# Attention values multiplied with tokens on partitions, normalised afterwards and transposed back, in a two-block transformer kernel

## The reference, cut to what matters

```python
q = apply_rope(rms_norm(q.reshape(B, T, 8, 64), qn_g), cos, sin)     # 8 heads of 64
k = apply_rope(rms_norm(k, kn_g), cos, sin)                          # one key head for all
score = einsum('bqhk,bqh->bqk', relu(q_idx . k_idx), w_idx * scale)  # the indexer
_, sel = lax.top_k(where(visible, score, NEG_INF), 64)
logits = einsum('bqhd,bqkd->bqhk', q, k[sel]) * 64 ** -0.5
p = softmax(where(valid, logits, NEG_INF), axis=-1)
attn = einsum('bqhk,bqkd->bqhd', p, v[sel])                          # one value head for all
y_a = einsum('bte,ed->btd', attn * silu(gate_a), w_a)
```

## Time and profile before

| | us |
|---|---|
| median of 3 runs | 1325.65 |
| lowest, highest | 1323.81, 1327.27 |
| the profiled execution | 1322.05 |
| its span | 1320.3 |
| PE busy | 1278.1 (97%) |
| PE weight loads busy | 1221.1 (92%) |
| POOL busy | 1007.3 (76%) |
| DVE busy | 694.1 (53%) |
| ACT busy | 668.7 (51%) |

### The profile page before, as it was taken

One profiled execution on the slowest core, in us unless ns is written; L12 is line 12 of the kernel. 1 busy time (PEld: TensorE's weight loads), 2 busy tenths in 40 slices (PEclk: granted clock), 3 DMA queues, 4 the chain that ended last, 5 costly groups with the idle time before them and its releaser, 6 DMA issues.

```text
span 1320.3 us, 24716 instructions
## 1 busy us (share of the span) xinstructions
PE 1278.1 (97%) x10187; PEld 1221.1 (92%) x10187; DVE 694.1 (53%) x1293; ACT 668.7 (51%) x1192; POOL 1007.3 (76%) x774
## 2 busy tenths in 40 slices
PE   6999999999999999999999998899999999999997
PEld 6988889988889999998999988899999889999997
DVE  5567647657656344411787688854145435344412
ACT  5455546455555544444555565565446445544532
POOL 4655658866559899987789866668899757899894
PEclk9999999999999999999999999999999999999999
DMA  6433435444335555555456533344556534555562
GB/s 234 144 117 124 128 113 174 153 138 144 116 117 192 170 191 188 189 184 186 130 165 201 163 119 123 126 130 158 182 188 216 165 103 154 177 191 181 186 193 79
DMA packets 57792, 209.05 MB, mean 158 GB/s; under 512 B 6352, under 2 KB 7632, under 8 KB 57424
## 3 DMA queue, kind: packets, MB, share of 16 engines
q1 hardware_dynamic: 57680, 207.48, 48.7%
HBM read 206.41 MB, written 1.05 MB: 157 GB/s over the span
## 4 chain that ended last, share of the span: by engine, by line
PE 86%; DVE 9%; ACT 2%; issue 1%; DMA 1%; SPq 0%; DVEq 0%
PE bank L338 26%; PE bank L340 25%; PE bank L339 25%; PE bank L802 2%; DVE ar L1546 1%; ACT whi L303 1%; PE bank L593 1%; PE bank L810 1%; DVE ar L1567 1%; DVE rows L395 1%; DVE ar L1680 1%; DVE ar L1696 1%; PE bank L817 1%; DMA raw<-w_dram 1%; PE bank L1988 1%
## 5 line engine op out<-in xcount | busy, mean ns | idle before, releaser
L311 POOL TENSOR_TENSOR wlo<-raw,whi 128x512 fp32r<-128x512 f32 x770 | 1007.1, 1339 | 296.7 <-ACT whi L303 296.3
L338 PE MATMUL bank<-xh,whi 128*128 128x256 f32 (+1 forms) x2024 | 586.4, 290 | 15.1 <-DVE xl L377 10.2
L340 PE MATMUL bank<-xh,wlo 128*128 128x256 f32 (+1 forms) x2024 | 575.8, 284 | 0.0
L339 PE MATMUL bank<-xl,whi 128*128 128x256 f32 (+1 forms) x2024 | 575.5, 284 | 0.0
L303 ACT ACTIVATE whi<-raw 128x1024 fp32r<-128x1024 f32 x387 | 399.0, 1049 | 40.4 <-DMA raw<-w_dram 20.2
L338 PEld LDWEIGHTS bank<-xh,whi 128*128 128x128 f32 x2024 | 386.5, 191 | 24.7 <-issue 15.2
L340 PEld LDWEIGHTS bank<-xh,wlo 128*128 128x128 f32 x2024 | 386.9, 191 | 0.0
L339 PEld LDWEIGHTS bank<-xl,whi 128*128 128x128 f32 x2024 | 385.7, 191 | 0.5
L338 PE MATMUL bank<-yh,whi 128*128 128x256 f32 (+1 forms) x1000 | 286.0, 286 | 0.3 <-DVE yl L1870 0.3
L340 PE MATMUL bank<-yh,wlo 128*128 128x256 f32 (+1 forms) x1000 | 283.6, 284 | 0.0
L339 PE MATMUL bank<-yl,whi 128*128 128x256 f32 (+1 forms) x1000 | 283.4, 283 | 0.0
(11 more groups left out here) (245 smaller groups left out, 1169.3 us busy)
## 6 DMA issues: line engine op xcount, KB each, us to landing
raw<-w_dram SPq DMA_DIRECT2D x387, 512.0 KB, 3.8
h<-x_dram SPq DMA_DIRECT2D x2, 544.0 KB, 6.4
cst<-con_dram SPq DMA_DIRECT2D x1, 1049.0 KB, 10.6
ar<-mem_dram SPq DMA_DIRECT2D x1, 1024.0 KB, 5.9
out_dram<-h SPq DMA_DIRECT2D x4, 256.0 KB, 2.7
cst<-con_dram SPq DMA_DIRECT2D x1, 134.0 KB, 3.8
prm<-par_dram SPq DMA_DIRECT2D x1, 131.0 KB, 4.4
```

Of the source, the lines that this page charges most:

```text
L311: return e.tensor_tensor(wlo[:, q, c0:c1], raw[:, i % NRAW, c0:c1], whi[:, q, c0:c1].bitcast(F), ALU.subtract)
L338: e.matmul(o, wh, xhi, start=(i == 0), stop=False)
L339: e.matmul(o, wh, xlo, start=False, stop=False)
L340: m = e.matmul(o, wl, xhi, start=False, stop=(i == len(feed) - 1))
```

## The change

Values and probabilities swap roles in the product: the transposed probabilities are the stationary operand (128 columns), the values the moving one (64 columns), and the output has the 128 query tokens on partitions and all eight heads side by side in the 512 columns of one bank. The probabilities are no longer multiplied by the reciprocals; one DVE operation divides the 128x512 result by the sums (a reciprocal of 8 columns, broadcast over 64), into the new buffer `K.o`. PE transposes that in four 128x128 blocks into a bank `oT`; one DVE operation multiplies by the gate in place in PSUM, one ACT copy makes the high part, one DVE subtraction the low part. Since the transposes of the probabilities wait for the exponential alone, transposes and value products both move one step earlier.

```diff
@@ attend_tensor
         for s in range(8):
-            if s == 4:
+            if s == 3:
                 ob = side_.take(e, "ob", l, t)
-            for hh in (range(2 * s - 8, 2 * s - 6) if s >= 4 else ()):
-                pt, half = K.PT.at(l, t, hh), 64 * (hh % 2)
+            for hh in (range(2 * s - 6, 2 * s - 4) if 3 <= s < 7 else ()):
+                pt = K.PT.at(l, t, hh)
                 e.wait_ge(*s_out.of("pt", l, t, hh))
                 for i, (vi, _, kn) in enumerate(kcs):
-                    m = e.matmul(ob[half:half + 64, 128 * (hh // 2):128 * (hh // 2) + 128], K.V[0:kn, vi, 0:64],
-                                 pt[0:kn, i, :], start=(i == 0), stop=(i == nn - 1))
+                    m = e.matmul(ob[:, 64 * hh:64 * hh + 64], pt[0:kn, i, :], K.V[0:kn, vi, 0:64], start=(i == 0),
+                                 stop=(i == nn - 1))
                 m.then_inc(*piece.done("av", l, t, hh))
-            for hh in (range(2 * s - 6, 2 * s - 4) if 3 <= s < 7 else ()):
+            for hh in (range(2 * s - 4, 2 * s - 2) if 2 <= s < 6 else ()):
                 o = side_.take(e, "pT", l, t, hh)
                 side_.give(("pT", l, t, hh), (s_out, ("pt", l, t, hh)))
-                e.wait_ge(*v_step.of("p", l, t, hh))
+                e.wait_ge(*s_step.of("exp", l, t, hh))
...
+            if s == 7:
+                side_.give(("ob", l, t), (v_step, ("o", l, t)))
+                o = side_.take(e, "oT", l, t)
+                side_.give(("oT", l, t), (v_low, ("y", l, t)))
+                e.wait_ge(*v_step.of("o", l, t))
+                for b in range(4):
+                    m = e.transpose(o[:, 128 * b:128 * b + 128], K.o[:, 128 * b:128 * b + 128], ident)
+                m.then_inc(*piece.done("oT", l, t))
             yield
-        side_.give(("ob", l, t), (v_step, ("y", l, t, 3)))
@@ attend_scalar
-            for hh in (2 * s - 6, 2 * s - 5) if 3 <= s < 7 else ():
+            for hh in (2 * s - 4, 2 * s - 3) if 2 <= s < 6 else ():
                 pt, o = K.PT.take(e, l, t, hh), side_.at("pT", l, t, hh)
...
-        for b in range(4):
-            y, _ = K.y(b, 0)
-            e.wait_ge(*v_step.of("y", l, t, b))
-            e.activation(y[:, c0:c0 + 128], K.tmp.at("y", l, t, b)[:, 0:128], ACT.Copy).then_inc(*s_high.done("y", l, t, b))
+        e.wait_ge(*v_step.of("y", l, t))
+        e.activation(K.y4(0, c0), side_.at("oT", l, t).rearrange("p (a b) -> p a b", b=128), ACT.Copy).then_inc(
+            *s_high.done("y", l, t))
@@ attend_vector
-            if 2 <= s < 6:
-                hs = slice(2 * s - 4, 2 * s - 2)
-                e.wait_ge(*s_step.of("exp", l, t, 2 * s - 3))
-                e.reciprocal(K.rs[:, hs], K.sm[:, hs]).then_inc(*v_step.done("rs", l, t, s - 2))
-                e.wait_ge(*v_step.of("rs", l, t, s - 2))
-                for hh in (2 * s - 4, 2 * s - 3):
-                    x = K.L[:, hh, 0:nk]
-                    e.tensor_scalar(x, x, K.rs[:, hh:hh + 1], None, ALU.mult).then_inc(*v_step.done("p", l, t, hh))
+            if s == 5:
+                e.wait_ge(*s_step.of("exp", l, t, 7))
+                e.reciprocal(K.rs, K.sm).then_inc(*v_step.done("rs", l, t))
...
+            if s == 6:
+                e.wait_ge(*piece.of("av", l, t, 7))
+                e.wait_ge(*v_step.of("rs", l, t))
+                e.tensor_tensor(K.o.rearrange("p (h d) -> p h d", d=64),
+                                side_.at("ob", l, t).rearrange("p (h d) -> p h d", d=64),
+                                K.rs.unsqueeze(2).broadcast_to([128, 8, 64]), ALU.mult).then_inc(*v_step.done("o", l, t))
+            if s == 7:
+                o = side_.at("oT", l, t).rearrange("p (a b) -> p a b", b=128)
+                e.wait_ge(*piece.of("oT", l, t))
+                e.wait_ge(*v_step.of("ga", l, 3))
+                e.scalar_tensor_tensor(o, o, 0.5, K.ga[:, :, c0:c0 + 128], ALU.mult, ALU.mult).then_inc(
+                    *v_step.done("y", l, t))
             yield
-        ob = side_.at("ob", l, t)
-        for b in range(4):
...
-        attend_low(e, K, t, 3)
+        e.wait_ge(*s_high.of("y", l, t))
+        e.tensor_tensor(K.y4(1, c0), side_.at("oT", l, t).rearrange("p (a b) -> p a b", b=128),
+                        K.y4(0, c0).bitcast(F), ALU.subtract).then_inc(*v_low.done("y", l, t))
```

More of the change, by code:

```diff
@@ L546, in __init__ @@
             (self.qT, self.qiT, self.kT, self.kiT, self.V, self.ga, self.gb, self.mg, self.L, scr0, scr1, pt0, pt1,
-             ra0, ra1, rg0, rg1, ub, tmp0, tmp1, self.m8, self.nm, self.sm, self.rs, self.psh) = arena(
+             ra0, ra1, rg0, rg1, ub, tmp0, tmp1, self.m8, self.nm, self.sm, self.rs, self.psh, self.o) = arena(
                 (4, T), (4, T), (T,), (T,), (3, 72), (4, T), (4, T), (16, T), (8, T), (T,), (T,), (3, 128), (3, 128),
-                (T,), (T,), (T,), (T,), (16 + T,), (T,), (T,), (8, 8), (8,), (8,), (8,), (4,))
+                (T,), (T,), (T,), (T,), (16 + T,), (T,), (T,), (8, 8), (8,), (8,), (8,), (4,), (512,))
             self.scr = [scr0, scr1]
@@ L563, in y, with y4 @@
             return yh[:, i * T + q0:(i + 1) * T], yl[:, i * T + q0:(i + 1) * T]
+        def y4(self, i, c0):
+            return (yh, yl)[i][:, 0:4 * T].rearrange("p (j t) -> p j t", t=T)[:, :, c0:c0 + 128]
         def keys(self, t):
@@ L869, in attend_vector @@
                                        ALU.add).then_inc(*v_step.done("qk", l, t, hh))
-            yield
-        ob = side_.at("ob", l, t)
-        for b in range(4):
[L873 to L880, removed]
-        attend_low(e, K, t, 3)
[L883 to L888, removed]
+            if s == 6:
[10 more added lines that the diff above has]
+                    *v_step.done("y", l, t))
+            yield
+        e.wait_ge(*s_high.of("y", l, t))
+        e.tensor_tensor(K.y4(1, c0), side_.at("oT", l, t).rearrange("p (a b) -> p a b", b=128),
+                        K.y4(0, c0).bitcast(F), ALU.subtract).then_inc(*v_low.done("y", l, t))
     def meta_tensor(e, K):
@@ L1150, in layer_tensor @@
             e.wait_ge(*v_low.of("my", l))
-        e.wait_ge(*v_low.of("y", l, 0, 3))
-        src = [(*K.y(g), ("y", l, 1, g)) for g in range(4)]
+        e.wait_ge(*v_low.of("y", l, 0))
+        src = [(*K.y(g), ("y", l, 1)) for g in range(4)]
         for b in range(8):
```

## The result

| | us |
|---|---|
| before, median of 5 runs | 1325.91 (1323.81 to 1327.27) |
| changed, median of 5 runs | 1331.34 (1330.90 to 1333.07) |
| ratio | 1.0045, 95% interval 1.0030 to 1.0059 |
| profiled executions, before and changed | 1322.05 and 1331.34 (spans 1320.3 and 1329.5) |

The forecast was 1330.2 us in 1322 to 1335. The sum in it was +4.5 us; the medians say +5.4, the two profiled executions +9.3. The experiments ask where these parts come from.

What follows compares the result with a forecast made beforehand. PE, busy for 97% of the span, was taken to bound the kernel. PE work +0.5 us and bank-ring stalls +4.0 us gave +4.5 us on the median of 1325.65: 1330.2 us, range 1322 to 1335.

Steps and rivals of the forecast that it cites:

- DVE and ACT count for nothing by themselves: Both layers' attention: removed multiplications and merged operations hide behind PE's stream; 0 us, apart from stalls.
- wait of PE for the transposes of `o`: End of each query tile, step 7: new wait taken as 0, about 1 us once if the cover failed.
- A value product costs 0.36 us in either form: PE's 80 value products: 0.36 us each before and after, so 0; bounds 8 us saved or lost.
- Rival (a): PE's value products: halved streams save 0.05 us on each of 160 passes, 8 us; 1322 us in all; chance 0.10.
- (d): PE's value products: a weight load costs in full, +12.5 us, 1338 us in all; chance 0.04.
- PE's other work +0.5 us: PE without stalls: group ends -1.4, transposes back +1.75, run-out -0.36, six switches +0.5; in all +0.5 us.
- Step 3, layer 0, t=0: PE's logits wait for a bank until ACT copies the step's first transpose: new stall of 2.2 us.
- Step 2, t=0: Both layers: six takes on four banks, logits wait for L775; 1.35 us each, +2.7 us together (1.5 to 3.5).
- Step 3, t=1: Both layers: PE waits for ACT's copy, 0.4 us each, +0.8 us together (0 to 2).
- Step 3, layer 1, t=0: The existing 2.1 us stall goes, a 0.4 us wait for ACT's copy comes; net -1.7 us.
- rival (c): Stalls drop PE's clock to half speed, +1.7 us per drop; up to +8 us, 1333.5 us; chance 0.11.

Runs made afterwards that it cites:

- b_nomul: The kernel before with the 32 multiplications of the probabilities (L861) left out, values not divided by the sums; 1322.21 us, ratio 0.9982.
- x_late: The changed kernel with the old steps for transposes, value products and the take of ob, transposes back in a ninth step; 1322.42 us, ratio 0.9977.
- x_share: The changed kernel with the transposes of a pair of heads in one bank for t=0, where there were two; 1325.13 us, ratio 1.0000.
- b_ob3: The kernel before with only the take of the bank for ob moved from step 4 to step 3; 1340.03 us, ratio 1.0116.
- x_order: The changed kernel with the key chunks of the first head of a pair taken in reverse; 1326.81 us, ratio 1.0003.
- x_rounds: The changed kernel with DVE's top-64 search rounds of t=1 moved behind the maximum of the logits; 1327.12 us, ratio 1.0007.
- b_order: The kernel before with the key chunks of the first head of a pair taken in reverse; 1318.92 us, ratio 0.9952.

## Why the prediction was right, step by step

- **DVE and ACT count for nothing by themselves**: right. DVE had 19 us less (25 to 30 forecast) and PE's chain was no shorter for it; b_nomul gained 0.7 us in the layers. No wait of PE for the transposes of `o` was seen.
- **A value product costs 0.36 us in either form**: right. The groups take 1.36 us (127.34 to 128.70) where the sum had 1.35, next to 1.44. Rival (a), which had the halved streams pay, and (d) are out. By the Trainium skill, "TensorE: Matmul & The Clock Gate", LDWEIGHTS, a load lasts with the number of its columns and not its rows. The traces agree: the second load of a product starts 0.11 us after the first in the changed kernel, with 16 rows and with 128, and 0.05 us after it in the kernel before, where a load has 64 columns.
- **PE's other work +0.5 us**: right in size. x_late measured 0.4 us, but with the old steps it lacks the six switches (0.5) that were all of the forecast's sum, so its own share of the sum was 0.0.
- **Step 3, layer 0, t=0: +2.2 us**: right in cause and nearly in size. The tick is 5.51 against 2.78 in x_share, which has the same work and no stall: 2.7, some of it at half speed. The idle time in PE's records is less, 1.7, as these begin when the modelled end of the matmul before is over.
- **Step 2, t=0: +1.35 each**: right. 3.37, less 1.35 and the transposes' 0.63, leaves 1.39.
- **Step 3, t=1: +0.4 each**: right. The tick of 4.08 holds the old one of 1.76 and value products of 1.80, with an entry that is 0.09 longer; 0.4 are left.
- **Step 3, layer 1, t=0: the old stall of 2.1 goes, 0.4 comes**: right. The tick fell by 0.34 us although it holds 1.35 us more work: -1.7.
- **The clock**: the part that I gave 0.11 as rival (c) came true beside the forecast and not in its place. The argument against it, that a stall of 2.1 us in layer 1 had left the clock alone, was from one case and too weak. b_ob3 has a slightly longer stall at the same place (1.6 us where it was 1.4), with PE busy for all of the 4 us ahead of it as in the kernel before, and there the clock fell. So thinner work around the stall is not needed for a drop, and what decides is open. In the layers' clock of the twelve profiles only the changed kernel and x_order (7 us each), which share the stall of step 3, and b_ob3 (17 us) have half-speed time. The drop cost 2.0 us in the blocks (x_rounds) and, as an estimate, the 0.5 us by which the tick exceeds the forecast; with 4.5 + 2.0 + 0.5, 0.3 of the layers' 7.3 us are left over.
- **The number** is closer than its terms, and that is luck in part. The sum of +4.5 us left out about 2.5 us of half speed, and against the median the step was smaller than in the layers, 5.4 and not 7.3. Why it was smaller is not shown. Half-speed stretches elsewhere in the program last longer in some executions than in others: by the clock of the twelve profiles they take 25 to 32 us outside the layers (26 in the kernel before, 28 in the changed one), and eleven runs of the kernel before, with mean clocks of 0.984 to 0.992, took 1321.9 to 1327.4 us. A step of 2 us is within that scatter in a single execution, and that is a reason to price a step in the profile between two fixed points.

## What to carry to other kernels

Where one engine's order is written out and its buffers come from a ring, count the takes of each step, together with what is held out of the ring: moving work one step earlier cost more than the arithmetic it belonged to. When a bound engine makes small products of different row counts, put equal ones side by side: the order of the chunks saved 5.6 us of the layers in the old form and 4.3 to 5.0 in the new one, 0.3 to 0.4% of the kernel. Read the records even where the gain is the expected one: two forms gained alike here for two different reasons. And a stall of 2 us on TensorE may be paid twice, once as the wait and once at half speed.

## What the runs showed of the hardware that was not expected

- Between small fp32 products of 16 and 128 rows TensorE stands for longer than at the entry from a block, 0.14 us against 0.09: reversing one head's chunks saved 0.34 us for each group of four products, where 0.18 was expected.
- Two 16-row products of 64 output partitions each, one for the lower and one for the upper half, ran at the same time once they stood side by side: four weight loads in the 0.19 us of two, and 0.35 us less for the group (b_order). With a 128-row product between them they did not.
- A half-speed stretch followed a stall of 1.7 us with thin work before it (130.0 to 137.1, clock 0.52), and the stalls of 3.2 and 2.6 us in b_ob3 (0.54, 0.58); none followed the stall of 1.4 us in the earlier trace rows, with PE busy on both sides, but one (0.50) followed a stall of 1.6 us at the same place in b_ob3, with PE as busy ahead of it.
